# The shared expert's down projection in four pieces inside the expert passes of a mixture-of-experts block

## The reference, cut to what matters

```
def moe_ffn(h, p):
    ...
    idx, w = route(xf, p["w_router"], p["router_bias"])          # 4 of 32 experts for each token
    comb = jnp.sum(jax.nn.one_hot(idx, N_EXPERTS, dtype=jnp.float32) * w[..., None], axis=1)
    g = jnp.einsum("td,edf->tef", xf, p["w_exp_gate"])           # (256, 2048) x (32, 2048, 256)
    u = jnp.einsum("td,edf->tef", xf, p["w_exp_up"])
    a = jax.nn.silu(g) * u * comb[..., None].astype(xf.dtype)
    routed = jnp.einsum("tef,efd->td", a, p["w_exp_down"])       # (32, 256, 2048)
    shared = (jax.nn.silu(xf @ p["w_sh_gate"]) * (xf @ p["w_sh_up"])) @ p["w_sh_down"]   # (512, 2048)
    return (routed + shared).reshape(shp)
...
h_new = h_new + gf_x * moe_ffn(modulated_norm(h_new, p["ffn_norm"], sf_x, scf_x), p)
```

## Time and profile before

| what | us |
|---|---|
| median of 3 runs | 1192.2 |
| lowest, highest | 1190.43, 1193.07 |
| the profiled execution, its time | 1190.26 |
| its span, first to last instruction | 1188.5 |
| PE busy in the span | 1034.8 (87%) |
| DVE, ACT busy | 560.5, 224.6 |
| mean rate of all transfers | 320 GB/s |

### The profile page before, as it was taken

The page is one execution under the profiler, slowest core; times in us unless marked ns, Lnnn a source line. Parts: engine busy times, 40 slices in busy tenths (PEclk is TensorE's granted clock), DMA queues, the critical chain, the costliest instruction groups (busy, mean ns, idle before and its releaser), DMA issues.

```text
span 1188.5 us, 15731 instructions
## 1 busy us (share of the span) xinstructions
PE 1034.8 (87%) x6018; PEld 576.8 (49%) x6031; DVE 560.5 (47%) x1114; ACT 224.6 (19%) x455; POOL 9.0 (1%) x13
## 2 busy tenths in 40 slices
PE   1879999999999998999799997879877987798773
PEld 0525568888875455444488443334333433243321
DVE  1300176865716684885352444444352455245415
ACT  4311110000002452000410021122122122122204
POOL 0000000000000000000000000000000000000002
PEclk9979999999999999999899999999998999999987
DMA  9998979999737618998606399999999999999992
GB/s 336 345 370 321 338 245 356 371 349 323 260 116 247 218 66 289 376 342 305 249 5 236 132 400 395 410 409 409 409 408 408 409 408 409 408 408 409 409 403 93
DMA packets 154710, 380.29 MB, mean 320 GB/s; under 512 B 12226, under 2 KB 43792, under 8 KB 151952
## 3 DMA queue, kind: packets, MB, share of 16 engines
q1 hardware_dynamic: 154640, 379.35, 85.2%
HBM read 377.22 MB, written 2.10 MB: 319 GB/s over the span
## 4 chain that ended last, share of the span: by engine, by line
PE 67%; DMA 14%; DVE 8%; SPq 6%; ACT 3%; issue 2%; ACTq 0%; POOL 0%; DVEq 0%
PE ps L566 65%; DMA ring<-in_w_exp_down 11%; SPq L492 4%; DMA ring<-in_w_mod 4%; DVE xres L1789 3%; DVE nreg L1753 1%; ACT nreg L1052 1%; DVE nreg L1783 1%; DVE part L1779 1%; SPq L373 1%; SPq L365 0%; DVE tiny L1532 0%; PE ps L636 0%; PE ps L811 0%; ACT ring L1206 0%
## 5 line engine op out<-in xcount | busy, mean ns | idle before, releaser
L566 PE MATMUL ps<-nreg,ring 128*128 128x256 f32 (+1 forms) x1280 | 300.1, 394 | 8.6 <-ACT nreg L1052 5.9
L566 PEld LDWEIGHTS ps<-nreg,ring 128*128 128x128 f32 x1280 | 242.9, 192 | 61.9 <-issue 20.2
L566 PE MATMUL ps<-ring,nreg 128*32 128x512 f32 (+1 forms) x1344 | 179.4, 626 | 24.6 <-DMA ring<-in_w_exp_up 24.6
L1384 DVE SCALAR_TENSOR_TENSOR part<-ring,csT,part 128x512 f32<-128x512 f32 x232 | 174.4, 752 | 8.9
L566 PE MATMUL ps<-ring,conv 128*32 128x512 f32 (+1 forms) x672 | 94.7, 648 | 31.7 <-DMA ring<-in_w_exp_down 31.2
L566 PEld LDWEIGHTS ps<-ring,nreg 128*32 128x32 f32 (+1 forms) x1344 | 52.5, 118 | 142.5 <-issue 142.5
L566 PE MATMUL ps<-ring 128*128 128x512 f32 x256 | 110.8, 592 | 0.0
L566 PE MATMUL ps<-nreg,conv 128*128 128x512 bf16 x252 | 64.1, 378 | 31.3 <-DVE xres L1789 30.6
L1767 DVE SCALAR_TENSOR_TENSOR conv<-ps,tiny,conv 128x256 f32<-128x256 f32 x12 | 5.8, 484 | 168.0 <-ACT conv L1246 168.0
L566 PEld LDWEIGHTS ps<-ring 128*128 128x128 f32 x256 | 48.6, 190 | 60.4 <-issue 60.3
L1789 DVE TENSOR_TENSOR xres<-xres,ps 128x512 f32<-128x512 f32 x96 | 61.5, 682 | 22.3 <-PE ps L566 22.2
(11 more groups left out here) (224 smaller groups left out, 891.7 us busy)
## 6 DMA issues: line engine op xcount, KB each, us to landing
ring<-in_w_mod SPq DMA_DIRECT2D x88, 1024.0 KB, 9.5
ring<-in_w_exp_gate SPq DMA_DIRECT2D x128, 512.0 KB, 13.4
ring<-in_w_exp_up SPq DMA_DIRECT2D x128, 512.0 KB, 15.5
ring<-in_w_exp_down SPq DMA_DIRECT2D x128, 512.0 KB, 13.5
ring<-in_w_in SPq DMA_DIRECT2D x15, 2048.0 KB, 11.2
ring<-in_w_out SPq DMA_DIRECT2D x8, 2048.0 KB, 10.7
ring<-in_w_mod SPq DMA_DIRECT2D x4, 2048.0 KB, 19.7
ring<-in_w_sh_gate SPq DMA_DIRECT2D x2, 2048.0 KB, 9.5
```

Of the source, the lines that this page charges most:

```text
L566: return nc.tensor.matmul(o, l, r, start=start, stop=stop)
L1384: ins = V.scalar_tensor_tensor(out=out_, in0=w_, scalar=scale, in1=acc_, op0=ALU.mult, op1=ALU.add)
```

## The change

The shared down projection is no longer a stage of its own ahead of the passes. Its weights become four more units of the ring, one for each block of 512 columns (all 512 rows of it: 1 MB). DOWN = {1: 0, 4: 1, 7: 2, 10: 3} puts the blocks into the T passes 1, 4, 7 and 10, where the unit is loaded and used between the third and the fourth quarter of gate and up. There PE runs shared_down, eight matmuls of 128x512 into banks 4 and 5, DVE gates them (shared_gated) and adds them to xres (shared_add). RING starts with slot 5, which nothing of the shared expert uses now, and first_room follows the new order. In the last pass the order is down 0 and 1, scatter 0 and 1, down 2 and 3, scatter 2 and 3; before, all four downs came ahead of the scatters. DVE's adds move with them.

```diff
@@ -46,7 +46,8 @@
+DOWN = {1: 0, 4: 1, 7: 2, 10: 3}
+BASES = [sum(6 * EXPERTS[kind] + (j in DOWN) for j, (kind, _) in enumerate(PASSES[:t])) for t in range(len(PASSES))]
@@ -162,7 +163,7 @@
-        RING = (2, 3, 4, 0, 5, 1)
+        RING = (5, 1, 2, 3, 4, 0)
@@ -474,9 +471,6 @@
             load_shared_up(3, su, 1)
-            load_shared_down(0)
-            sp.wait_ge(sh_gate, 4)
-            load_shared_down(1)
@@ -493,27 +487,37 @@
+            def load_shared_down(n, m):
+                for c in range(2):
+                    sp.dma_start(unit(n)[:, 1024 * c:1024 * c + 1024].rearrange("p (c n) -> p c n", c=2),
+                                 sd[:, 2 * c:2 * c + 2, 512 * m:512 * m + 512]).then_inc(unit_in[n % UNITS], 16)
+
             def first_room(n):
-                if n == 0:
+                if n == 2:
                     sp.wait_ge(sh_gate, 4)
-                elif n == 2:
+                elif n == 6:
                     sp.wait_ge(hT_full, 8)
                     sp.wait_ge(split_ready, 2)
-                elif n == 4:
+                elif n == 8:
                     sp.wait_ge(sh_up, 4)
-                elif n == 8:
-                    sp.wait_ge(sh_down, 8)
...
                 for stage in range(6):
+                    if stage == 3 and t in DOWN:
+                        room(n)
+                        load_shared_down(n, DOWN[t])
+                        n += 1
                     for e in experts:
...
@@ -924,20 +928,8 @@
             gather(0, (0, 1))
             pe.wait_ge(rank_ready, 1)
-            for s, use in SH_DOWN:
-                pe.wait_ge(w_full[s], 16 * use)
-            for j in range(8):
...
-                    ins = mm(ps[:, 4 + m, :], shT[k][:, 128 * t:128 * t + 128], w[:, k % 2, 512 * m:512 * m + 512],
-                             k == 0, k == 3)
-                ins.then_inc(sh_down, 1)
             gather(0, (2, 3))
+            pe.wait_ge(sh_act, 4)
@@ -947,10 +939,25 @@
+            def shared_down(t, n):
+
+                wait_units((n,))
+                if t:
+                    pe.wait_ge(y_gate, 4 * t)
+                w = unit(n).rearrange("p (c n) -> p c n", c=4)
+                for h in range(2):
+                    for c in range(4):
+                        ins = mm(ps[:, 4 + h, :], shT[c][:, 128 * h:128 * h + 128], w[:, c, :], c == 0, c == 3)
+                    ins.then_inc(sh_down, 1)
+
...
+                    if shared and q == 3:
+                        shared_down(t, first)
+                        first += 1
...
+                            if shared and q == 3 and k == at == 0:
+                                ins.then_inc(unit_used, 1)
@@ -982,9 +991,12 @@
+                shared = kind != "over" and t in DOWN
+                if shared:
+                    pe.wait_ge(sh_gated, 2 * DOWN[t] + 2)
...
@@ -1003,26 +1015,34 @@
                 pe.wait_ge(pickT_out, t + 1)
-                if ahead:
-                    gather(t + 1, (2,), last)
+                if not ahead:
+                    for n in range(2):
+                        down(n)
+                    for n in range(2):
+                        scatter(n)
+                    for n in range(2, 4):
+                        down(n)
+                    for n in range(2, 4):
+                        scatter(n)
+                    return
+                for n in range(4):
+                    down(n)
+                gather(t + 1, (2,), last)
                 scatter(0)
...
@@ -1711,14 +1731,18 @@
+            def shared_gated(m):
+                for h in range(2):
+                    ve.wait_ge(sh_down, 2 * m + h + 1)
+                    V.tensor_tensor(ygate[:, h, :], ps[:, 4 + h, :], gfB[:, 512 * m:512 * m + 512], ALU.mult)\
+                        .then_inc(sh_gated, 1)
+
+            def shared_add(m):
+                cols = slice(512 * m, 512 * m + 512)
+                for h in range(2):
+                    ve.wait_ge(sh_gated, 2 * m + h + 1)
+                    ins = V.tensor_tensor(xres[:, h, cols], xres[:, h, cols], ygate[:, h, :], ALU.add)
+                link(ins)
@@ -1762,6 +1786,9 @@
                     weighted_picks(*ahead)
+                if not over and t in DOWN:
+                    shared_gated(DOWN[t])
+                    shared_add(DOWN[t])
                 ve.wait_ge(weight_ready, t + 1)
@@ -1794,21 +1821,28 @@
                 lowest(0)
                 rest(1)
-                gated(2)
+                if not (last or over):
+                    gated(2)
                 lowest(1)
+                if last or over:
+                    add(0)
+                    gated(2)
+                    add(1)
...
@@ -1816,11 +1850,8 @@
             tokens_out(0, 1)
+            tokens_out(0, 3)
             ve.wait_ge(modT_done, 24)
-            for m in range(8):
-                shared_out(m)
-            tokens_out(0, 3)
-            ve.wait_ge(y_add, 8)
```

More of the change, by code:

```diff
@@ L48 @@
           ("T", 7))
-BASES = [6 * sum(EXPERTS[kind] for kind, _ in PASSES[:t]) for t in range(len(PASSES))]
+DOWN = {1: 0, 4: 1, 7: 2, 10: 3}
+BASES = [sum(6 * EXPERTS[kind] + (j in DOWN) for j, (kind, _) in enumerate(PASSES[:t])) for t in range(len(PASSES))]
 OVER = ((1, 0, 96, 2), (14, 1, 64, 2), (16, 15, 32, 1))
@@ L463, in load_shared_up @@
                   .then_inc(w_full[s], 16)
-            def load_shared_down(half):
-                s = SH_DOWN[half][0]
-                sp.dma_start(k_of(s, 2), sd[:, 2 * half:2 * half + 2, :]).then_inc(w_full[s], 16)
             sp.wait_ge(wo_full, 3)
@@ L984, in expert_pass, with down @@
                 pe.wait_ge(actT_out, t + 1)
-                for n in range(4):
-                    first = base + EXPERTS[kind] * (4 + n // 2)
+                shared = kind != "over" and t in DOWN
+                if shared:
+                    pe.wait_ge(sh_gated, 2 * DOWN[t] + 2)
+                def down(n):
+                    first = base + EXPERTS[kind] * (4 + n // 2) + shared
                     if n % 2 == 0 and kind != "over":
@@ L1005, in scatter @@
                         if kind == "over":
+                            pe.wait_ge(y_add, 8 * t + (max(m - 1, 0) - 8))
+                        elif not ahead and m >= 2:
+                            pe.wait_ge(fin_h, m - 1)
+                        elif t or m >= 2:
                             pe.wait_ge(y_add, 8 * t + max(m - 1, 0))
-                        elif ahead or m < 2:
-                            pe.wait_ge(y_add, 8 * t + (8 + max(m - 1, 0)))
-                        else:
-                            pe.wait_ge(fin_h, m - 1)
                         for a in range(3):
@@ L1801, in pair_pass @@
                 lowest(2)
-                add(0)
+                if not (last or over):
+                    add(0)
                 rest(3)
                 lowest(3)
-                add(1)
+                if not (last or over):
+                    add(1)
                 if ahead:
@@ L1810, in pair_pass @@
                 if not last:
-                    ve.wait_ge(y_add, 8 * t + (8 if over else 16))
+                    ve.wait_ge(y_add, 8 * t + (0 if over else 8))
             ve.wait_ge(rank_ready, 1)
```

34 lines of the change are left out of this document (9 added, 25 removed).

## The result

| kernel | median, us | lowest, highest | ratio to before, 95% interval |
|---|---|---|---|
| before | 1191.32 | 1189.29, 1193.07 | |
| after | 1172.32 | 1171.53, 1175.52 | 0.9846 [0.9821, 0.9872] |

A forecast was written before the change was run, and what follows sets the result against it. From about 680 us the expert-weight transfers were taken to set the pace. Terms -27.0 + 10.3 + 0.5 - 1.8 = -18.0 us took 1190.3 to 1172.3 profiled, 1174 us forecast for the median, range 1168 to 1182.

The forecast's parts named there:

- Pass 0 earlier: Start of the passes: without the shared down stage ahead, pass 0 begins at 655.5 instead of 682.55, 27.0 us earlier.
- The stream follows: Weight stream after pass 0 starts: eight units landed before 650, unit 24 released at 694.4, again 27.0 us earlier.
- The gap that was to be 2.6 us: Ahead of unit 24: the stream, started 30.07 us earlier, stands idle some 2.6 us.
- What is left to move: Stream from unit 24 on: four more units cost +10.3 us, their 2 KB rows +0.5.
- The bound of 2.8 us: Upper bound on the cost of 2 KB rows, at 321 GB/s, the lowest busy slice of the first half.
- Pieces on PE: Passes 1, 4, 7, 10: 6.87 us a piece costs nothing, under 14.2 us of waiting per T, T, P group.
- Pieces on DVE: Gating and adding a piece is hidden before the fourth quarter: 0 us, at worst 2 us each.
- The tail: Last pass: two scatters ahead of down 2 gain 1.8 us, 14.4 in place of 16.2, full clock assumed.
- (d): Rival: PE becomes the bound of the passes, a piece costing 26 us; at 30 us, 1206 us; chance 0.02.
- (e): Rival: something else holds pass 0 until 682, giving 1201 us; chance 0.02.
- (b): Rival: part is lost in the stream by longer idle at unit 24 or slow 2 KB pieces; 1178 to 1186; chance 0.12.
- (c): Rival: more is gained, last pass -4 and less stream idle; 1166 to 1169 us; chance 0.08.

The follow-up runs named there:

- the late pass: Kernel after with 32 more unused matmuls of 128x512 ahead of gather(0, (2, 3)), so pass 0 starts late: 1198.67 us, ratio 1.0067.
- the run again: The kernel after, unchanged, measured a second time: 1170.32 us, ratio 0.984 to the kernel before.
- T passes first: Kernel after with two T passes ahead of the S pass, P passes and pieces moved to suit, run twice: 1170.94 us (0.9848) and 1169.93 us (0.984).

## Why the prediction was right

**Pass 0 earlier** (-27.0): measured -26.8 against the end of the shared gate and up. The rest of the start's shift, 2.2 us, is none of the prediction's: the end of gate and up itself lay earlier. So the predicted terms came to -16.4 where -18.0 was forecast, and that the whole trace shows -18.6 is in part luck. The 2.2 us more likely belong to the execution than to the change: with the order of after the end lies between 645.98 and 650.63 in twelve traces, and in four of these PE runs slow behind its idle stretch as long as in the two with the order of before (650.00 and 650.85). Two traces of before are too few to settle it. The pass's late start costs its length (the late pass: 26 us for 27.3), and early loads without it nothing.

**The stream follows** (unit 24 again 27.0 earlier): it is 38.99 us behind pass 0, 38.85 before. The gap that was to be 2.6 us is 2.2, at 690 to 696 as foretold. (The prediction gives no working for 2.6; its own 30.07 and 27.0 us differ by 3.1. Its sum doesn't use it.) The order of the ring was needed for it; the prediction had that in its count of units at 650, without a price, and the price is about half of the gain by the times, 6.3 us of it in the stream by the trace.

**What is left to move** (+10.3 + 0.5): +11.5 in the trace, 10.7 in that of the run again, and 10 to 12 us by the kernel without these loads. The four units pay their bytes, and for the rows of 2 KB the window from 680 to 690 gives an estimate of 0.9 to 1.5 us where the prediction has 0.5. The lower rate from 696 on is there without them too, and from 720 on it is 406 after, 408 in the run again and 408 without the loads, 409 before. (The bound of 2.8 us took 321 GB/s as the lowest busy slice; lower ones, such as 289 and 305, stand in the earlier trace rows too. Nothing hangs on it.) The Trainium skill (DMA: Bandwidth & Descriptors, Measured) wants 1 MiB or more in a transfer for 75% of peak and gives 341 GB/s for 1 MB, for transfers that GpSimd issues. Here SP issues transfers of 512 KB, the pieces' too, many of them under way, and the flat part runs at 406: its figure doesn't carry over to this stream.

**Pieces on PE** (nothing, cover 14.2 us): between once, twice and not at all no difference can be measured, four times takes 47 us more. The cover was read from passes T, T, P as the difference of stream and PE, and the waits bear the direction out: 57.6, 38.4, 19.1. They also show a thing that the prediction's reading of the waits left out: it counted 31.2 us for down weights as where PE stops, while PE stopped another 24.6 us for gate and up.

**Pieces on DVE** (hidden). DVE's timeline after, through the first piece:

```profile
702.84 0.69 DVE L1737 TENSOR_TENSOR nreg<-ps,qkv 128x512 f32<-128x512 f32 x1 [10.36 <-PE ps L570]
...
706.27 0.69 DVE L1737 TENSOR_TENSOR nreg<-ps,qkv 128x512 f32<-128x512 f32 x1 [2.74 <-PE ps L570]
706.88 1.28 DVE L1744 TENSOR_TENSOR xres<-xres,nreg 128x512 f32<-128x512 f32 x2
...
710.39 0.48 DVE L1794 SCALAR_TENSOR_TENSOR conv<-ps,tiny,conv 128x256 f32<-128x256 f32 x1 [2.23 <-ACT conv L1266]
```

The piece's adds end at 708.16, DVE then waits 2.23 us for the fourth quarter by way of ACT.

**The tail** (-1.8): -1.2. Its steps came as written: down 2 started 2.7 us after its weights (predicted 2.8), the last add ended 14.4 us after they landed (14.4), and down 0 to the last add is 1.74 us shorter. The span's end gave 0.5 us back between the last add and the last store, for no cause that the traces show. The choice of full clock was luck in part: from 1142 to 1158 the granted clock is 1.00 after, but in seven of eleven traces with this last pass it fell, and the stretch was up to 1.7 us longer than the 22.99 of before. No timed comparison of this term reaches beyond its uncertainty; it rests on the traces where the clock stayed.

**The rivals.** (d), PE as the bound, was rightly put far away: a piece of 13.7 us costs nothing that can be measured, 27.5 us makes 1.0224. Its price was too low, though: it put 1206 us at a piece of 30 us, and 1219 were measured at 27.5, as the stream stops at a full ring. (e), pass 0 held by something else, is out by 653.51. (b) and (c) would have been 1178 or more and 1169 or less; the medians of the two runs of the kernel after, 1172.32 and 1170.32, are between them.

## What to carry to other kernels

Where a ring of buffers is full before its consumer starts, the stream is tied to the consumer: move the consumer's start, and the end moves with it, while loads issued earlier give nothing. Once the consumer starts early this turns round: then each unit that could be loaded ahead counts, and with four fewer of them about half of the gain was lost. A stage in front of such a stream can be cut up and put under the consumer's waits for free until its work exceeds what the stream leaves, but its bytes then pay the stream's full rate (10 to 12 us for 4.2 MB here). Before a gap in the stream is worked at, look whether the stream and the consumer would only wait elsewhere; with T passes first they did.

## What I had not expected of the hardware

The time at which the same work ends differs by 4.7 us between executions of nearly the same kernel (645.98 to 650.63 at the end of the shared gate and up, in the twelve traces with the order of after). PE is idle there from about 575 to 580, and two things make up the difference. The first matmul behind the idle stretch itself starts between 578.2 and 581.1; for that no cause is seen. And from there to the end it takes 67.6 to 68.1 us in eight of the traces, and 69.5 or 69.6 in four. This second part goes with the moment at which the granted clock comes back. The second row of matmuls behind the idle stretch, in the kernel before and after:

```profile
584.46 3.65 PE L859 MATMUL ps<-cst,ring 128*128 128x128 f32 x16 [0.62 <-ACT nreg L1213]
...
584.22 2.19 PE L863 MATMUL ps<-cst,ring 128*128 128x128 f32 x16 [0.62 <-ACT nreg L1233]
```

A window of the kernel before:

```profile
586.00:590.00 4.00, 4.00 (x42) 2.70 (x40) 1.99 (x4) 1.62 (x4) 0.00 (x0) 0.64 0.00 0
```

0.64 against the 1.00 of the kernel after (the first row of its windows above) in the same four microseconds, in a part of the program that the change doesn't touch; the kernel before with the new tail, which ends gate and up at 650.85, has 0.59 there. The trace of before takes 69.8 us over this part and that of after 67.8, which is 2.0 of the 2.2 us in the first row of the table of parts. A single trace of a change worth 2 us can't be read without looking at this. The link is seen side by side in traces; no run set the clock by itself.
